# Tiles on x times the norm's weight, six more gate tiles as split products, and an earlier gather for the first expert job

## What is computed

```
for l in 0, 1:
    h = rmsnorm(x, norm1_g[l]);  p = h @ W_in[l]
    yA = conformer_conv(p_glu)              # GLU, causal depthwise conv (31), LayerNorm, silu, projection
    yB = gated_deltanet(p_qkv, p_z, p_a, p_b)
    x = x + (sigmoid(p_gA) * yA + sigmoid(p_gB) * yB) @ W_o[l]
    h2 = rmsnorm(x, norm2_g[l])
    x = x + (swiglu(h2) if l == 0 else top_2_of_8_swiglu_experts(h2))
y = rmsnorm(x, final_g)
```

## Time and profile before

| | us |
|---|---|
| median of 3 runs | 1614.76 (1613.64 to 1615.12) |
| the profiled execution | 1613.09 |
| its span | 1611.3 |
| TensorE busy | 1563.1 (97%) |
| VectorE busy | 1208.5 (75%) |
| ScalarE busy | 924.6 (57%) |
| granted TensorE clock, mean | 0.983 |

### The profile page before, as it was taken

One profiled execution on the slowest core, in us unless ns is written; L12 is line 12 of the kernel. 1 busy time (PEld: TensorE's weight loads), 2 busy tenths in 40 slices (PEclk: granted clock), 3 DMA queues, 4 the chain that ended last, 5 costly groups with the idle time before them and its releaser, 6 DMA issues.

```text
span 1611.3 us, 30488 instructions
## 1 busy us (share of the span) xinstructions
PE 1563.1 (97%) x10847; PEld 1404.5 (87%) x10847; DVE 1208.5 (75%) x1731; ACT 924.6 (57%) x1284; POOL 37.6 (2%) x52
## 2 busy tenths in 40 slices
PE   6999999899998999999989999999999999999997
PEld 4989977799987889986789798998979889798995
DVE  4788945555301688884489998989989899998987
ACT  4643332444201563251277787777877778777775
POOL 0000002000000000000040000000000000000000
PEclk9999899899999999989999999999999999999999
DMA  6652135766445553213669999999999999999993
GB/s 244 191 124 66 41 111 194 292 183 183 131 144 166 184 147 85 73 59 109 245 240 379 389 352 369 357 361 352 357 384 344 363 363 358 369 356 366 351 370 119
DMA packets 108893, 397.50 MB, mean 247 GB/s; under 512 B 13601, under 2 KB 13648, under 8 KB 108176
## 3 DMA queue, kind: packets, MB, share of 16 engines
q1 hardware_dynamic: 104464, 376.23, 66.4%
q0 software_dynamic: 4352, 20.20, 3.5%
HBM read 380.94 MB, written 16.43 MB: 247 GB/s over the span
## 4 chain that ended last, share of the span: by engine, by line
PE 91%; DVE 7%; ACT 1%; DMA 1%; issue 1%; SPq 0%; DVEq 0%; ACTq 0%
PE psum L1334 67%; PE psum L1602 5%; PE psum L1367 4%; DVE c L944 3%; PE psum L1547 2%; PE psum L1549 2%; PE psum L1440 1%; PE psum L1448 1%; PE psum L1556 1%; PE psum L1702 1%; PE psum L1452 1%; PE psum L1376 1%; PE psum L1406 1%; DMA ring<-in_w_mixer 1%; DVE w_lo L843 1%; PE psum L1637 1%
## 5 line engine op out<-in xcount | busy, mean ns | idle before, releaser
L1334 PE MATMUL psum<-w_hi,h_hi 128*96 128x256 f32 x1408 | 399.7, 284 | 0.1
L1334 PE MATMUL psum<-w_hi,h_lo 128*96 128x256 f32 x1408 | 394.5, 280 | 0.0
L1334 PE MATMUL psum<-w_lo,h_hi 128*96 128x256 f32 x1408 | 393.7, 280 | 0.0
L1272 DVE TENSOR_TENSOR w_lo<-ring,w_hi 128x1024 fp32r<-128x1024 f32 x288 | 346.9, 1221 | 37.1 <-ACT w_hi L796 35.2
L796 ACT ACTIVATE w_hi<-ring 128x1024 fp32r<-128x1024 f32 x288 | 303.6, 1058 | 42.9 <-PE psum L1334 33.9
L1334 PE MATMUL psum<-hid_hi,w_hi 128*128 128x264 f32 x992 | 288.3, 291 | 8.4 <-DVE hid_lo L849 6.1
L1334 PE MATMUL psum<-hid_lo,w_hi 128*128 128x264 f32 x992 | 282.8, 285 | 0.0
L1334 PE MATMUL psum<-hid_hi,w_lo 128*128 128x264 f32 x992 | 282.5, 285 | 0.0
L1272 DVE TENSOR_TENSOR w_lo<-early,w_hi 128x1024 fp32r<-128x1024 f32 x192 | 231.3, 1221 | 18.2 <-ACT w_hi L796 18.2
L1334 PEld LDWEIGHTS psum<-w_hi,h_hi 128*96 128x96 f32 x1408 | 228.1, 162 | 0.8 <-DVE w_lo L1272 0.3
L1334 PEld LDWEIGHTS psum<-w_hi,h_lo 128*96 128x96 f32 x1408 | 228.5, 162 | 0.0
(11 more groups left out here) (314 smaller groups left out, 1889.5 us busy)
## 6 DMA issues: line engine op xcount, KB each, us to landing
ring<-in_w_exp SPq DMA_DIRECT2D x288, 512.0 KB, 5.5
early<-in_w_exp SPq DMA_DIRECT2D x192, 512.0 KB, 5.4
ring<-in_w_mixer SPq DMA_DIRECT2D x112, 512.0 KB, 3.7
ring<-in_w_ffn SPq DMA_DIRECT2D x66, 512.0 KB, 3.6
qkv<-in_w_exp SPq DMA_DIRECT2D x48, 512.0 KB
h_rows<-work POOLq DMA_DIRECT2D x12, 480.0 KB, 14.3
early<-in_s POOLq DMA_DIRECT2D x2, 2048.0 KB, 7.9
out_ss<-early POOLq DMA_DIRECT2D x2, 2048.0 KB, 9.7
```

Of the source, the lines that this page charges most:

```text
L1272: V.tensor_tensor(w_lo[:, buffer_x(u), :], slot_x(u % RING_X), w_hi[:, buffer_x(u), :], ALU.subtract).then_inc(lo_done, 1)
L1334: last = M(out, lhs[x], rhs[w], start=(start and n == 0), stop=(stop and n == 2))
```

## The change

1. `x_gain` = x times the norm's weight (VectorE, into `qkv`'s memory) is made before the root is known. Tiles 0 and 1 of each mixer layer, the a and b products, and tiles 0 and 1 of the dense feed-forward are plain products on `x_gain`, and their results are multiplied by `rstd` afterwards on VectorE.
2. The sums of squares are interleaved with the matmuls ahead of them where x is made (last output tiles of layer 0, last blocks of the down projection), as are layer 1's a and b products; the high and low parts of the first split tiles are moved forward, and `glu(0)` ahead of the gating values.
3. x is loaded in two halves behind the constants and parameters.
4. `PLAIN` is {0, 1}: tiles 34 to 39 are split; their high parts follow the gates on ScalarE, their low parts are put between VectorE's taps and norms.
5. Routing: `take` for job 0 is made from the ranks of expert 0 alone; the rest of the routing runs in three portions at units 4, 7 and 9 of job 0.

```diff
-PLAIN = {0, 1, 34, 35, 36, 37, 38, 39}
+PLAIN = {0, 1}
...
+        x_gain = qkv[:, 0:KD, :]
+        ab_row = work[0:2 * H, 7, 0:T]
...
-                               ("ffn", range(2 * FT)),
+                               ("ffn", range(2, 2 * FT)),
...
-            sp.dma_start(xT[:, :, :].rearrange("p k t -> p (k t)"), a["xT"]).then_inc(x_loaded, 16)
             sp.dma_start(consts[:, :, :].rearrange("p k t -> p (k t)"), a["consts"]).then_inc(consts_loaded, 16)
             sp.dma_start(prm[:, :], a["params"]).then_inc(consts_loaded, 16)
+            for i in range(2):
+                sp.dma_start(xT[:, i * 4:i * 4 + 4, :].rearrange("p k t -> p (k t)"), a["xT"][:, i * 4 * T:(i + 1) * 4 * T]).then_inc(x_loaded[i], 16)
...
# ScalarE
-                model_squares(2 * l)
                 if l == 0:
                     act.wait_ge(consts_loaded, 32)
-                for i in range(2, 2 + LEAD):
-                    high_part(section, i)
-                model_rms(2 * l)
+                    model_squares(0)
+                    model_rms(0)
+                    high_part(section, 2)
+                    high_part(section, 3)
+                else:
+                    model_squares(2, 0, 6)
+                    high_part(section, 2)
+                    model_squares(2, 6, 7)
+                    high_part(section, 3)
+                    model_squares(2, 7, 8)
+                    model_rms(2)
+                high_part(section, 4)
...
-                        if GATE_AT + t + LEAD < min(i for i in PLAIN if i > 1):
+                        if GATE_AT + t + LEAD < N_PROJ:
                             high_part(section, GATE_AT + t + LEAD)
...
-                    model_rms(2 * l + 1)
-                    high_part("ffn", 0)
+                    model_squares(1, 0, 6)
+                    high_part("ffn", 2)
+                    model_squares(1, 6, 8)
+                    model_rms(1)
+                    high_part("ffn", 3)
...
# VectorE
+            def gain(stage, k, g_name, g_at):
+                V.tensor_scalar(x_gain[:, k, :], xT[:, k, :], par(g_name, g_at + k), None, ALU.mult).then_inc(x_gain_done, 1)
+            def norm_parts(l2, split_stage):
+                for k in range(KD):
+                    V.tensor_tensor(hT[:, k, :], x_gain[:, k, :], rstd[:, :], ALU.mult).then_inc(h_done, 1)
+                    if k:
+                        x_low(split_stage, k - 1)
+                x_low(split_stage, KD - 1)
...
-                for k in range(KD):
-                    V.scalar_tensor_tensor(hT[:, k, :], xT[:, k, :], par("norm1", l * KD + k), rstd[:, :], ALU.mult, ALU.mult).then_inc(h_done, 1)
-                for k in range(KD):
-                    x_low(3 * l, k)
                 dve.wait_ge(ab_rows, l + 1)
-                V.tensor_copy(rstd[0:2 * H, :], psum[0:2 * H, 6, 0:T]).then_inc(ab_copied, 1)
-                for i in range(2, 2 + LEAD):
-                    low_part(section, i)
+                V.tensor_tensor(ab_row, psum[0:2 * H, 4, 0:T], rstd[0:2 * H, :], ALU.mult).then_inc(ab_copied, 1)
+                norm_parts(2 * l, 3 * l)
+                if l == 0:
+                    low_part(section, 2)
+                dve.wait_ge(units_used, base_ord[section] + 2)
+                V.tensor_tensor(glu_gate(0), psum[:, 1, 0:T], rstd[:, :], ALU.mult).then_inc(gate_scaled, 1)
+                if l == 0:
+                    low_part(section, 3)
...
-                        conv_taps(18, 27)
+                        conv_taps(18, 23)
+                        low_part(section, 34)
+                        conv_taps(23, 27)
+                        low_part(section, 35)
...
                 conv_taps(29, DW)
+                low_part(section, 36)
...
# routing, job 0
                     dve.wait_ge(ranks_mm, 1)
+                    settle(V.scalar_tensor_tensor(first_slot, psum[:, 5, 0:24:NE], 1.0, sent[:, 0:24:NE], ALU.add, ALU.mult))
+                    for m in range(3):
+                        ins = V.tensor_scalar(take[:, m, :], par("slot_row", 0, CAP), 1.0, first_slot[:, m:m + 1], ALU.add, ALU.is_equal)
+                    ins.then_inc(take_done, 1)
...
                                 h_low(0, 1)
-                                late_routing()
+                                token_rows()
+                            if first and u == SPLIT + 3:
+                                token_gates()
+                            if first and u == SPLIT + 5:
+                                job_list()
...
# TensorE
+                project(0)
+                project(1)
+                pe.wait_ge(ab_copied, l + 1)
...
                     if l == 0 and t == KD - 2:
+                        model_sums(1, 0, 4)
                 if l == 0:
-                    model_sums(1)
+                    model_sums(1, 4, KD)
+                    for i in range(2):
+                        w = arrived("ffn", i)
+                        for k in range(KD):
+                            pe.wait_ge(x_gain_done, KD + k + 1)
+                            last = M(psum[:, i, 0:T], w[:, k, :], x_gain[:, k, :], start=(k == 0), stop=(k == KD - 1))
...
+                        if f == FT - 1 and t >= 2:
+                            model_sums(2, t - 2, t - 1)
+                            ab_products(1, t - 2, t - 1)
+                    ab_products(1, KD - 2, KD - 1)
+                    model_sums(2, KD - 2, KD)
+                    ab_products(1, KD - 1, KD)
```

More of the change, by code:

```diff
@@ L236, in build @@
         units_used = sem("units_used")
-        x_loaded = sem("x_loaded")
+        x_loaded = [sem(f"x_loaded{i}") for i in range(2)]
         consts_loaded = sem("consts_loaded")
@@ L525, in _, with model_squares @@
             A = nc.scalar.activation
-            def model_squares(l2):
-                for k in range(KD):
-                    if k == 0:
-                        act.wait_ge(x_loaded, 16)
+            def model_squares(l2, k0=0, k1=KD):
+                for k in range(k0, k1):
+                    if l2 == 0 and k % 4 == 0:
+                        act.wait_ge(x_loaded[k // 4], 16)
                     if l2 % 2:
@@ L749, in _ @@
                         A(x_hi[:, k, :], hT[:, k, :], ACT.Copy).then_inc(x_hi_done, 1)
-                    for u in range(1, 2 * FT + 2):
+                    for u in range(4, 2 * FT + 2):
                         if u < 2 * FT:
@@ L1342, in split_tile, with model_sums, ab_products @@
                 return last
-            def model_sums(l2):
-                for k in range(KD):
+            def model_sums(l2, k0=0, k1=KD):
+                for k in range(k0, k1):
                     pe.wait_ge(squares_done, KD * l2 + k + 1)
                     last = M(psum[:, 5 if l2 < 2 * DEPTH else 3, 0:T], ones, sq[:, k, :], start=(k == 0), stop=(k == KD - 1))
-                last.then_inc(sums_done, 1)
+                if k1 == KD:
+                    last.then_inc(sums_done, 1)
+            def ab_products(l, k0=0, k1=KD):
+                for k in range(k0, k1):
+                    pe.wait_ge(x_gain_done, 2 * KD * l + k + 1)
+                    last = M(psum[0:2 * H, 4, 0:T], par_block("w_ab", l, KD * 8)[:, k * 8:(k + 1) * 8], x_gain[:, k, :], start=(k == 0), stop=(k == KD - 1))
+                if k1 == KD:
+                    last.then_inc(ab_rows, 1)
             pe.wait_ge(consts_loaded, 32)
@@ L1365, in project @@
                     if i in PLAIN:
+                        rhs = x_gain if i < 2 else hT
                         for k in range(KD):
-                            last = M(psum[:, i % 4, 0:T], w[:, k, :], hT[:, k, :], start=(k == 0), stop=(k == KD - 1))
+                            last = M(psum[:, i % 4, 0:T], w[:, k, :], rhs[:, k, :], start=(k == 0), stop=(k == KD - 1))
                     else:
@@ L1583, in _ @@
                             router_sum(k)
+                    if l == 0 and t == KD - 2:
+                        model_sums(1, 0, 4)
                 if l == 0:
-                    model_sums(1)
-                    for f in range(FT):
+                    model_sums(1, 4, KD)
+                    for i in range(2):
+                        w = arrived("ffn", i)
+                        for k in range(KD):
+                            pe.wait_ge(x_gain_done, KD + k + 1)
+                            last = M(psum[:, i, 0:T], w[:, k, :], x_gain[:, k, :], start=(k == 0), stop=(k == KD - 1))
+                        last.then_inc(units_used, 1)
+                    for f in range(1, FT):
                         if f >= 3:
@@ L1696, in job_units @@
                                 pe.wait_ge(chunk_done, job * NCH + (ch + 1))
+                                if ch == 1 and first:
+                                    pe.wait_ge(row_at_done, 1)
                                 if ch >= 2:
```

134 lines of the change are left out of this document (78 added, 56 removed).

## The result

The changed kernel takes **1596.0 us** (median of five runs, 1593.1 to 1602.9) against 1613.6 (1612.4 to 1615.1): ratio 0.9895, interval 0.9869 to 0.9921. On the profiled execution (1597.5 us, span 1595.7) the gain is 15.6 us of span.

A forecast was written before the change was run, and what follows sets the result against it. TensorE, busy 97% of the span, was taken as the bound, with idle holes to fill. Terms 9.3 + 10.3 + 5.7 + 1.2 + 4.6 = 31.1 us gave 1583.7 us, range 1577.5 to 1592.

The forecast's parts named there:

- What bounds the kernel: TensorE busy 97% of the span; only removing its work or filling its idle holes pays, each hole bringing slow clock behind it.
- clock 0.5 in the gates: Gates: one of the listed signs that would show the forecast wrong, TensorE's granted clock at 0.5 there.
- Part 1: Layer 0's start: x's first half lands at 7.5, tile 6 starts at 39.6 instead of 48.96; 9.3 us (6 to 11).
- Part 2: Feed-forward's start: plain tiles follow the sums without waiting for the root, tile 3 at 305.6 instead of 316.0; 10.3 us (8 to 11).
- Part 3: Layer 1's start: last x to gating rows takes 29.2 us plus 1.1 stall instead of 36.0; 5.7 us (3.5 to 7).
- Part 4: Tiles 34 to 39, both layers: TensorE saves 5.2 a layer, VectorE's low parts and clock take most; 1.2 us together.
- the first rival: Gates, both layers: VectorE's low parts make them slower, -1.4 a layer, 1587.7 to 1592.5, say 1590; chance 0.18.
- Part 5: Gather for job 0: ends at 814.2 instead of 820.25, less 1.4 for late low parts; 4.6 us (1.5 to 6.5).
- I take the clock as kept: Gather: with 1 us of hole instead of 4.4 the full clock stays, so 48 records take 5.8 us.
- the starts are not clean: Starts and gather: x late, low parts 2 to 5 late, or low clock in the gather; about 6 less, 1589.7; chance 0.17.
- the gates are slower: Gates, both layers: VectorE's low parts cost -1.4 a layer instead of gaining, say 1590 in all; chance 0.18.
- The ninth job: Experts' job loop: altered rounding gives one expert more than 96 tokens, so one more job runs, 1682; chance 0.02.

## Why the prediction was right and wrong, by its own steps

- **What bounds the kernel**: right about the holes, 10.3 of the 15.6 us came from shorter idle time. "After such a hole TensorE runs at the lower of its two levels" was only half of it: the trace of the kernel before already has half clock without a hole, for 10.3 us in each mixer layer, in no row of the prediction. Its sign of being wrong "clock 0.5 in the gates" could therefore not tell: it was there before the change.
- **Part 1** (9.3, measured 6.3, in the bounds). The step that failed is "I take the middle, 7.5" for x. With the constants first, its first half landed at 7.5 to 10.1 in the profiled runs, at 9.8 in this one; and the table load, which in the kernel before ran at 0.73 us, ahead of x, had been moved behind x with ScalarE's wait for the constants: 1.28 us that the prediction did not count. The first sum so came 4.1 us late, and the sums and the a, b products took 9.1 us instead of 9.9. In the run with x at 7.5 the kernel is 8.7 us ahead here. VectorE's pairs ended at 27.3 and low part 2 at 28.4, where the plain tiles ended at 28.1: that cover was judged right.
- **Part 2** (10.3, measured 4.7, outside 8 to 11). The step that failed is "the sums end at 295.2 as before: half of them move one tile forward, the work is the same". The work was; ScalarE's order was not. The high part of tile 2 was put ahead of squares 6 and 7, its weights came while 5.8 MB of zeros filled the DMA engines, and the prediction put that wait at nothing: 4.59 us, and half clock behind it. The trace of the kernel before has the engines full from 270 to 300 us, in no row of the prediction. With the stores spread the term measured 10.8. This is the largest miss, 5.6 us.
- **Part 3** (5.7, measured 5.1): right.
- **Part 4** (1.2, measured +1.1 and -1.6). The stall of 2.4 us for the copy was there in layer 1 (2.49), in layer 0 0.9. The clock was costed at 0.6 a layer; the runs with and without the edits show several stretches that cost 1.7 us each, some ahead of the edits. This is in part the first rival's mechanism (2.8 us of loss), and the term lies between it and the forecast.
- **Part 5** (4.6): 5.2 alone, 3.5 in company; "I take the clock as kept" was the step that did not hold in the changed kernel.
- **A term that wasn't there**: 3.1 us in layer 0's gating stretch, where TensorE was busy with unchanged instructions and ran two stretches of 3.4 us at half clock, 3.4 us lost. The same instructions kept the full clock in the kernel before, with the routing alone and in three other kernels. The prediction tied the low clock to holes; here it fell while TensorE was busy without a break, behind its 8-row products.
- **The rivals.** Of "the starts are not clean" (chance 0.17, 1589.7) x late and the gather's low clock came true, 4.1 us together; "the gates are slower" (0.18) came true by 1.7 of its 4.0 us. The two largest misses, the wait for tile 2's weights (5.6) and the clock in layer 0 (3.1), were in no rival. Without these two the time would have been some 1587, inside the range. The range took in one rival at a time. That 31.1 less 6, 4 and 3 is 18, near the measured 17.6, is chance. The ninth job did not come (x1408 as before); the slower side that did exist, a loop whose code is loaded again, was in no row of the kernel before but the count of instruction packets.

What stays open: what decides in which runs the clock falls in a stretch whose instructions are the same; what makes some places of the loop's code bad; and the two levels of the changed kernel's runs, 6 us apart.

## What to carry to other kernels

Whoever moves a copy that needs a weight tile ahead of work that TensorE waits for must look at the DMA share of that stretch: an engine that works its list in order, as ScalarE did at 293 us, hands a late load on to everything behind it, and bulk stores that nobody waits for could here be spread with no new wait of TensorE. Take a part's worth from a kernel with that part alone, but check the instruction packets of its queue first: a loop's code that is loaded again made one part look some 23 us worse than it is. Where several starts must mesh, their bad cases add. List the half-clock stretches of the kernel before, with what TensorE did ahead of each, before a low clock is tied to holes.

## What the runs showed of the hardware

- TensorE's job loop lost 9 to 10 us in a round when its code was loaded again (waits of up to 4.0 us, then half clock). It went with the number of instructions ahead of the loop: with 5029 and 5030 it came (in most runs, by their times), with 5061, 5093, 5158 and 5221 or more in no profiled one; and not in every run or round of the same program.
- The granted clock fell to 0.5 while TensorE was busy throughout, at unchanged instructions, in some kernels and not in others: for 3.4 us behind products over 8 rows (86.7 and 93.6 us), and for 6.8 to 13.7 us from inside 64 products of 2 columns on (178.9). All stretches at half clock together, those behind holes too, took 36 to 68 us ahead of 1590 us in the kernels without reloaded code, up to 16 us of time between the best and the worst.
- 64 instructions that only wait for a semaphore already reached delayed TensorE's first product by 4.2 us, from 7.45 to 11.70.
- At the start, x, constants and parameters were all in by 9.4 to 9.5 us with x first and by 9.9 and 11.4 with the constants first; holding back the weights changed nothing (9.54 and 9.35).
- Twelve stores of 480 KB on GpSimd's queue, issued at once beside the other transfers, kept the DMA share at 0.96 to 1.01 from 265 to 295 us, and ScalarE waited 10.72 us for a 512 KB weight tile; spread, the shares were 0.45 and 0.29 from 270 to 280 us and the wait 3.12 us.
